# Down projections as block products in Strassen's way, with the outputs summed in SBUF

## The reference

```
def swiglu(x, w_gu, w_down):
    g, u = jnp.split(x @ w_gu, 2, axis=-1)
    return (jax.nn.silu(g) * u) @ w_down
...
    f = swiglu(rmsnorm(h, g[N_FFN1_PRE]), ffn_w_gu[layer, 0], ffn_w_down[layer, 0])
    h = h + 0.5 * rmsnorm(f, g[N_FFN1_POST])
```

## Time and profile before

| | before |
|---|---|
| median of three executions | 2197.93 us |
| span of the profiled execution | 2196.3 us (its own time is not given apart from the span) |
| TensorE busy (matmul) | 2181.2 us, 99% |
| VectorE busy | 1456.1 us, 66% |
| ScalarE busy | 1127.0 us, 51% |
| weight stream and inputs | 221.44 MB, mean 101 GB/s |

### The profile page before, as it was taken

The page is one execution under the profiler, slowest core; times in us unless marked ns, Lnnn a source line. Parts: engine busy times, 40 slices in busy tenths (PEclk is TensorE's granted clock), DMA queues, the critical chain, the costliest instruction groups (busy, mean ns, idle before and its releaser), DMA issues.

```text
span 2196.3 us, 36637 instructions
## 1 busy us (share of the span) xinstructions
PE 2181.2 (99%) x13844; PEld 1944.0 (89%) x13844; DVE 1456.1 (66%) x2185; ACT 1127.0 (51%) x1881; POOL 110.4 (5%) x104
## 2 busy tenths in 40 slices
PE   9999999999999999999999999999999999999999
PEld 8999888775888899998899998887868889999987
DVE  8888636788666598874388885345266656888732
ACT  6555524476554565563365554245345546555531
POOL 0000000675000000000000000000000000000000
PEclk9999999999999999999999999999999999999999
DMA  4332332221452233332323323322214422333322
GB/s 164 105 105 95 115 106 63 77 77 49 144 165 79 74 115 105 105 105 96 115 87 105 105 95 115 115 81 87 96 36 138 155 79 77 103 105 105 110 99 78
DMA packets 61953, 221.44 MB, mean 101 GB/s; under 512 B 7953, under 2 KB 8081, under 8 KB 61858
## 3 DMA queue, kind: packets, MB, share of 16 engines
q1 hardware_dynamic: 57456, 208.69, 28.9%
q10 hardware_dynamic: 4402, 11.46, 1.5%
HBM read 218.03 MB, written 2.10 MB: 100 GB/s over the span
## 4 chain that ended last, share of the span: by engine, by line
PE 93%; DVE 4%; ACT 1%; POOL 1%; issue 1%; DMA 0%; DVEq 0%; POOLq 0%
PE ps L2099 12%; PE ps L2100 12%; PE ps L2101 12%; PE ps L2195 11%; PE ps L2197 11%; PE ps L2196 11%; PE ps L479 6%; PE ps L480 6%; PE ps L481 6%; PE ps L2035 1%; DVE e_sc L1768 1%; DVE e_max L1767 1%; DVE e_sc L1783 1%; PE ps L2583 0%; PE ps L2560 0%
## 5 line engine op out<-in xcount | busy, mean ns | idle before, releaser
L417 DVE TENSOR_TENSOR w_lo<-w_raw,w_hi 128x1024 fp32r<-128x1024 f32 x204 | 252.5, 1241 | 358.2 <-ACT w_hi L412 357.3
L412 ACT ACTIVATE w_hi<-w_raw 128x1024 fp32r<-128x1024 f32 x210 | 221.6, 1057 | 311.4 <-PE ps L2197 225.4
L2099 PE MATMUL ps<-t_hi,w_hi 128*128 128x256 f32 x1280 | 362.3, 283 | 0.0
L2100 PE MATMUL ps<-t_lo,w_hi 128*128 128x256 f32 x1280 | 362.2, 283 | 0.0
L2101 PE MATMUL ps<-t_hi,w_lo 128*128 128x256 f32 x1280 | 362.2, 283 | 0.0
L2099 PE MATMUL ps<-x_hi,w_hi 128*128 128x256 f32 x960 | 271.7, 283 | 0.0
L2100 PE MATMUL ps<-x_lo,w_hi 128*128 128x256 f32 x960 | 271.7, 283 | 0.0
L2101 PE MATMUL ps<-x_hi,w_lo 128*128 128x256 f32 x960 | 271.7, 283 | 0.0
L1490 DVE TENSOR_TENSOR w_lo<-f,w_hi 128x1024 fp32r<-128x1024 f32 x152 | 186.2, 1225 | 124.0 <-ACT w_hi L840 124.0
L479 PE MATMUL ps<-x_hi,w_hi 128*128 128x256 f32 (+1 forms) x736 | 250.8, 341 | 1.6 <-DVE x_lo L1367 0.9
L480 PE MATMUL ps<-x_lo,w_hi 128*128 128x256 f32 (+1 forms) x736 | 246.0, 334 | 0.0
(11 more groups left out here) (352 smaller groups left out, 4317.8 us busy)
## 6 DMA issues: line engine op xcount, KB each, us to landing
w_raw<-in_wstream SPq DMA_DIRECT2D x310, 512.0 KB, 3.3
w_raw_odd<-in_wstream SPq DMA_DIRECT2D x80, 512.0 KB, 3.3
tmp<-in_post_gains ACTq DMA_DIRECT2D x8, 512.0 KB, 5.1
gain_bc<-in_gains ACTq DMA_DIRECT2D x7, 512.0 KB, 3.8
h<-in_x SPq DMA_DIRECT2D x4, 512.0 KB, 5.7
c_mem<-in_mem ACTq DMA_DIRECT2D x2, 1024.0 KB, 5.8
out_dram<-h SPq DMA_DIRECT2D x3, 512.0 KB, 2.7
c_gain<-in_mem_gains ACTq DMA_DIRECT2D x2, 512.0 KB, 7.5
```

The source lines that it names most:

```text
L412: nc.scalar.activation(weights(v)[0], raw(v), ACT.Copy).then_inc(w_hi_ready, 1)
L417: nc.vector.tensor_tensor(wl, raw(v), wh.bitcast(f32), ALU.subtract).then_inc(w_ready, 1)
L2099: nc.tensor.matmul(dst, wh[:, at], xh[:, b, :], start=first, stop=False, skip_group_check=True)
L2100: nc.tensor.matmul(dst, wh[:, at], xl[:, b, :], start=False, stop=False, skip_group_check=True)
```

## The change

The first 12 of the 22 inner blocks are treated as a two by two block matrix: tokens in two halves of 256 (tiles 0 and 1, tiles 2 and 3), inner blocks in two halves of six, output columns in two halves of 512. Seven products of sums of blocks take the place of eight products. The other ten blocks are multiplied as before. In all a down stage has 31 units (21 for the seven products, 10 for the rest) where it had 22.

(Line numbers from here on are those of the changed kernel.) VectorE forms the sums: four sums over `act_raw` of 128x1536 (L1875, L1958, L1965, L1978) and twelve weight sums of 128x1024 (L1933, L1939, L1945, L1950). Units 0 to 30 are split as before, and a block product's activations are split with its unit, as 128x512 (`down_split`, L1894 and L1899). Three of the seven products are kept once and used for two or more outputs: ScalarE copies four accumulators from PSUM to `f` (`hold`), and VectorE adds the final accumulators to them there, in five sums (`sum_c`, L1905). Afterwards `post_square` and `store_half` read `f` in place of PSUM.

SyncE makes 34 loads of 512 KB in a down stage in place of 22, into ten raw places; six of these lie in the memory of `x_hi` and `x_lo` and can be loaded only when the gate and up stage has read its inputs. Ten of the loads stand in a row with few waits between them.

The late units are gone. Tiles 0 and 1 are complete together, before the last 72 matmuls of the stage; tile 2 and tile 3 end with units 28 to 30. VectorE and ScalarE split units 29 and 30, and the first four units of the next part, between the steps of the tiles' tail.

```diff
+HALF_K = 6
+DQ = HALF_K // 2
...
-    "ffn": [("gate_up", 2 * FT), ("down", FT)],
+    "ffn": [("gate_up", 2 * FT), ("down", 7 * DQ + 2 * (FT // 2 - 2 * DQ))],
...
+            d_x = early.enter_context(nc.sbuf_tensor("d_x", [P, 8, UW], f32))
...
+            d_a = part_sb("d_a", [P, 9, 4, SEQ // 2], f32r)
+            w_raw_odd = part_sb("w_raw_odd", [P, 2, UW])
...
+        FROM_RAW = {0: (0, 1), 1: (1, 1), 2: (2, 1), 3: (3, 1), 4: (X4, 1), 5: (X5, 1), 8: (1, 2), 11: (X4, 2),
+                    14: (0, 3), 15: (1, 3), 16: (2, 3), 20: (X4, 3), 21: (2, 4), 22: (X6, 3), 23: (3, 4), 24: (1, 4),
+                    25: (X5, 4), 26: (0, 5), 27: (X4, 4), 28: (X6, 4), 29: (3, 5), 30: (2, 5)}
+        FROM_T1, FROM_T2 = {6: 0, 9: 1, 13: 2}, {7: 0, 10: 1, 12: 2}
+        FROM_T3, FROM_T4 = {17: 0, 18: 1, 19: 2}, {28: 0, 29: 1, 30: 2}
+        A_OF = {0: (0, 0), 1: (2, 0), 2: (4, 0), 3: (6, 0), 4: (8, 0), 5: (10, 0), 6: (0, 1), 7: (0, 0), 9: (2, 1),
+                10: (2, 0), 12: (4, 0), 13: (4, 1), 17: (0, 1), 18: (2, 1), 19: (4, 1), 20: (6, 0), 22: (8, 0),
+                24: (10, 0), 28: (6, 1), 29: (8, 1), 30: (10, 1)}
+        A_SLOT = {k: (0, 3, 7, 1)[n % 4] for n, k in enumerate(sorted(A_OF))}
...
+                sp.wait_ge(w_ready, u0 + 2 * FT - 3 + 1)
+                load(0, B11)
+                load(1, B11 + 1)
+                sp.wait_ge(w_ready, u0 + 2 * FT - 1 + 1)
+                load(2, B11 + 2)
+                load(3, B21)
+                sp.wait_ge(prod, 5 * (SEVENS[i] + FT))
+                load(X4, B21 + 1)
+                load(X5, B21 + 2)
+                load(KEPT, B11)
+                load(X6, B12)
+                load(KEPT + 1, B11 + 1)
+                load(KEPT + 2, B11 + 2)
+                split(0)
+                load(0, B22)
+                split(1)
+                load(1, H0)
+                split(2)
+                load(2, B12 + 1)
+                split(3)
+                load(3, B22 + 1)
...
@@ ScalarE, norm(i) behind a down stage @@
+                elif parts[i - 1][0] == "ffn":
+                    u0 = U[i, UNITS[parts[i][0]][0][0]]
+                    post(i, 0)
+                    down_split(i - 1, 29)
+                    square(0)
+                    post(i, 1)
+                    down_split(i - 1, 30)
+                    square(1)
+                    split_hi(act, u0)
+                    post_square(i - 1, 0, 2)
+                    post_square(i - 1, 0, 3)
+                    upper(0)
+                    split_hi(act, u0 + 1)
+                    post_square(i - 1, 1, 2)
...
@@ VectorE, norm(i) behind a down stage @@
+                elif parts[i - 1][0] == "ffn":
+                    u0 = U[i, UNITS[parts[i][0]][0][0]]
+                    post(i, 0)
+                    update(i, 0)
+                    down_split(i - 1, 29)
+                    scale(0)
+                    post(i, 1)
+                    update(i, 1)
+                    down_split(i - 1, 30)
+                    scale(1)
+                    sum_c22(i - 1)
+                    split_lo(dve, u0)
+                    half_sums(i - 1, 2, 4)
+                    store_half(i - 1, 0, 2)
+                    store_half(i - 1, 0, 3)
+                    lower(0)
+                    sum_c21(i - 1, 2)
+                    split_lo(dve, u0 + 1)
+                    lower(1)
+                    post(i, 2)
+                    split_lo(dve, u0 + 2)
+                    update(i, 2)
+                    sum_c21(i - 1, 3)
+                    post(i, 3)
+                    split_lo(dve, u0 + 3)
+                    update(i, 3)
+                    scale(2)
+                    scale(3)
+                    lower(2)
...
@@ VectorE @@
+            def down_split(i, k):
+
+                v = U[i, "down"] + k
+                dve.wait_ge(w_hi_ready, v + 1)
+                if k in A_OF:
+                    hi, lo = split_a(k)
+                    nc.vector.tensor_tensor(lo, act_part(*A_OF[k]), hi.bitcast(f32), ALU.subtract)
+                elif k in PLAIN_A:
+                    raw_a, hi, lo = plain_a(PLAIN_A[k])
+                    nc.vector.tensor_tensor(lo, raw_a, hi.bitcast(f32), ALU.subtract)
+                wh, wl = weights(v)
+                nc.vector.tensor_tensor(wl, down_source(k), wh.bitcast(f32), ALU.subtract).then_inc(w_ready, 1)
+
+            def sum_c(i, b, tiles, half, kept):
+
+                dve.wait_ge(d_kept, 4 * nffn[i] + kept)
+                place = f[:, tiles, half * SEQ:(half + 1) * SEQ]
+                nc.vector.tensor_tensor(place, ps[:, b, :], place, ALU.add).then_inc(d_c, 1)
...
+                dve.wait_ge(d_s, c0 + 1)
+                read(2)
+                nc.vector.tensor_tensor(a11, a21, a11, ALU.subtract).then_inc(d_s, 1)
+                down_split(i, 4)
+                first_form(0, X6, 1)
+                down_split(i, 5)
+                second_form(0, 0, 2)
+                dve.wait_ge(d_s, c0 + 2)
+                read(5)
+                nc.vector.tensor_tensor(a12, a12, a11, ALU.subtract).then_inc(d_s, 1)
+                first_form(1, 2, 2)
+                down_split(i, 6)
+                second_form(1, 3, 2)
+                down_split(i, 7)
+                down_split(i, 8)
+                read(6)
+                first_form(2, X5, 2)
+                down_split(i, 9)
+                second_form(2, X6, 2)
+                for k in range(10, 14):
...
+                for k in range(26, 29):
+                    down_split(i, k)
+                dve.wait_ge(d_full, 2 * nffn[i] + 1)
+                sum_c(i, slice(0, 2), slice(0, 2), 1, 2)
...
@@ TensorE @@
+                pe.wait_ge(g_sum, 2 * (s0 + FT - 2) + 3)
+                unit(0)
+                strassen(0, 6, start=True).then_inc(w_free, 1)
...
+                unit(6)
+                strassen(6, 0, start=True).then_inc(w_free, 1)
+                held(1)
+                unit(7)
+                strassen(7, 6).then_inc(w_free, 1)
+                unit(8)
+                plain(8, 0, (0, 1), (4, 5))
+                plain(8, 0, (2, 3), (2, 3), start=True).then_inc(w_free, 1)
...
+                unit(25)
+                plain(25, 2, (0, 1), (0, 1))
+                unit(26)
+                plain(26, 3, (0, 1), (0, 1))
+                unit(27)
+                plain(27, 4, (0, 1), (0, 1), stop=True).then_inc(d_full, 1)
+                plain(25, 2, (2, 3), (6, 7)).then_inc(w_free, 1)
+                plain(26, 3, (2, 3), (6, 7)).then_inc(w_free, 1)
+                plain(27, 4, (2, 3), (6, 7), stop=True).then_inc(w_free, 1)
+                unit(28)
+                strassen(28, 2, (0,))
+                unit(29)
+                strassen(29, 2, (0,))
+                unit(30)
+                strassen(30, 2, (0,), stop=True).then_inc(d_full, 1)
+                if i + 1 < NP:
+                    turn_x(i + 1, 0)
+                strassen(28, 2, (1,)).then_inc(w_free, 1)
+                strassen(29, 2, (1,)).then_inc(w_free, 1)
+                if i + 1 < NP:
+                    turn_x(i + 1, 1)
+                strassen(30, 2, (1,), stop=True).then_inc(w_free, 1)
 
             def output(i, seg, nu, src_hi, src_lo, halves=(0, 1), tile_ready=None):
 
```

More of the change, by code:

```diff
@@ L229, in trunk @@
         u_sum = sem("u_sum")
-        act_ready = sem("act_ready")
+        d_in = [sem(f"d_in{n}") for n in range(10)]
+        d_s = sem("d_s")
+        d_t = sem("d_t")
+        d_kept = sem("d_kept")
+        d_full = sem("d_full")
+        d_c = sem("d_c")
         o_full = sem("o_full")
@@ L477, in three, with o_half @@
+        def o_half(i, s, t):
+            return 1 - s if parts[i][0] == "ffn" and t >= 2 else s
+        NOUT = [i - nffn[i] for i in range(NP)]
+        SUMMED, n = [], 0
+        for i in range(NP):
+            first, both = (1, 2) if parts[i][0] == "ffn" else (1, 1)
+            SUMMED.append((n + first, n + both))
+            n += 0 if feeds_selection(i + 1) else both
         def three(dst, wh, wl, xh, xl, start, stop):
@@ L705, in post_mean @@
                 else:
-                    act.wait_ge(half_ssq, sum(not feeds_selection(k) for k in range(1, i + 1)))
-                    act.wait_ge(o_sq, TT * (2 * i - 1) + t + 1)
+                    act.wait_ge(half_ssq, SUMMED[i - 1][t // 2])
+                    act.wait_ge(o_sq, o_index(i - 1, 1, t) + 1)
                     bias = stat[:, i, t:t + 1]
@@ L787, in norm @@
                     whole(1)
+                    whole(2)
+                    upper(3)
+                    whole(3)
+                elif parts[i - 1][0] == "ffn":
[12 more added lines that the diff above has]
+                    post_square(i - 1, 1, 2)
+                    upper(1)
+                    post_mean(i, 2)
+                    split_hi(act, u0 + 2)
+                    post(i, 3)
+                    split_hi(act, u0 + 3)
+                    whole(0)
+                    square(2)
+                    whole(1, (0,))
```

(15 more changed lines are left out.)

423 lines of the change are left out of this document (354 added, 69 removed).

## The result

The changed kernel takes **2205.76 us** (median of 6 runs, 2203.65 to 2210.36) against 2197.94 before (6 runs, 2197.74 to 2198.49): a ratio of 1.0039, 95% interval 1.0027 to 1.0050. It is slower, by 7.8 us, and its runs spread over 6.7 us where those of before spread over 0.8. The forecast was 2193.2, the range ended at 2201. The profiled execution has a span of 2203.5 us at a mean granted clock of 0.994.

What follows compares the result with a forecast made beforehand. The prediction took TensorE, busy 99% of the span, to bound the kernel. Of 32.6 us saved, 24.3 were given back and 3.6 went to the clock, leaving 4.7: 2197.9 - 4.7 = 2193.2 us, range 2187 to 2201.

Steps and rivals of the forecast that it cites:

- What the change removes: TensorE in the four down stages: 36 of 528 matmuls fewer per stage, 8.15 us each, 32.6 us in all.
- First units: Start of each down stage: TensorE waits 0.4 us for unit 6 and 0.15 for unit 7, 0.5 per stage.
- Loads: Row of loads at a down stage's start: no cost up to 1.43 us each; ninth there at 12.5, needed at 13.7.
- Rival 3: First units' sums wait for loads: each 0.1 us per load over 1.43 costs 0.9 us per stage; chance 0.12.
- Tail behind part 0: End of the first down stage: TensorE waits 1.6, 1.6 and 5.7 us, so the stage's gain is 0.0.
- Tail behind parts 3 and 4: Ends of these down stages: TensorE's waits, first units included, come to 7.0 us, gain 1.1 us each.
- Part 7: Last down stage, with no next part: 119.3 us long against 125.3 before, gain 6.0 us.
- The clock: Behind the three third-transpose gaps: the granted clock falls, costing 1.2 us each, 3.6 us in all.
- rival 4: Low clock lasts twice as long, or also follows 1.6 us waits: 3.4 us per tail, 2199.8 us; chance 0.18.
- The sum: Whole kernel: 32.6 us saved, 24.3 given back, 3.6 for the clock, 4.7 left; span 2191.6, median 2193.2 us.

Runs made afterwards that it cites:

- last version: Changed kernel with post gains' load later, third unit's first half earlier, tail reordered, unit 29's split moved, and C12 (an output quarter) finished tile by tile: 2174.20 us.
- The fillers: Unused matmuls ahead of the third tile's transposes behind parts 0, 3 and 4, added to the changed kernel with the post gains' load late: 2194.92 us.

## Why the prediction was wrong, point by point

- **What the change removes**, 144 matmuls, 32.6 us: right. The last version keeps 23.7 us of it.
- **First units**, 0.5 us per stage: right for VectorE's own work. With the gain load late, the early waits are 0.6 and 0.8 us in two stages and 0.2 in two (tile-by-tile kernel). The 128x1536 sum took 1.67 us from start to start (243.81 to 245.48, L1958) against the 1.68 by the slope.
- **Loads: the step that failed.** "The loads cost nothing up to 1.43 us each" counted the weight loads in SP's queue and no other. The post gains' load on ScalarE's queue falls between them, and the weights that VectorE needed came 1.09 us late. The ninth load of the row, reckoned at 12.5 us into the stage, is what VectorE waits for until 15.65. With the gains late it is still 14.13, against a sum that could have begun at 13.7, just as predicted. So of the 3.1 us by which the load is late, 1.5 are the post gains', about the place of one more load, and 1.6 belong to the row of weight loads itself. Measured, TensorE waits 2.3, 1.2, 1.2 and 2.0 us for 0.5 each; the load's price is 5.6 us in the changed kernel and 6.4 in the last version. Rival 3 named the right place, the sums waiting for the row of loads. By the same reckoning (a start at -1.2, 2.0 for the first, nine loads) the weights alone came at 1.48 us each, past the border of 1.43, and with the post gains among them at 1.65. Why the weights alone took 1.48 and not the 1.3 of the opening stays open.
- **Tail behind part 0**: right. Waits of 1.5, 1.6 and 5.5 us at unit 30, first half unit and third transpose against 1.6, 1.6 and 5.7; the chain 32.9 us against 32.75. It began 3.6 us late, by the early wait (2.3 for 0.5) and the low clock behind it (1.7 us lost).
- **Tail behind parts 3 and 4**: near. Predicted 0.7 + 1.3 + 4.5; measured 0.5 + 1.8 + 2.8 and 0.5 + 1.8 + 4.3.
- **Part 7**: 121.5 us against 119.3 predicted; 1.5 of the 2.2 us is the early wait.
- **The clock: the second step that failed**, in size. I took 1.2 us for each of three gaps. The rows give 9.5 us of lost work in five stretches: 7.8 in the four at the tails, where I had 3.6, and 1.7 behind an early wait, where I had allowed for none. The fillers measured 5.2 us for the three tails with the load late. My reason for 1.2 and not 1.7, that part of the slow stretch lies in the gap, is true of part 0 (6.8 us low, 3.4 of them in the wait) and of part 4 (6.8 us low, 1.3 of them in the wait). But those stretches were twice as long as the one in the earlier trace rows, and behind part 3 a second one came, 0.7 us behind a first half unit that had waited 1.8 us. Both are what rival 4 named. The fillers' kernel kept a granted clock of 1.00, 2.4 GHz, by work that nobody uses. The rule of the Trainium skill (TensorE: Matmul & The Clock Gate, Part 1: The HAM clock gate), that the throttled state is the default and activity lifts it, agrees with that.
- **The sum.** 2203.5 against the 2191.6 of the working is 11.9 us: early waits +4.7, clock +5.9, tail waits -1.6; that leaves 2.9. The fall at 526.3 us that the kernel before has and this execution has not counts 1.7 the other way, so 4.6 us have to be placed. About 2.5 of them lie around the seven waits for a unit, which cost TensorE more than the idle time that the profile gives. One of 1.2 us, in part 3:

```profile
999.85 0.39 PE L2556 MATMUL ps<-w_hi,d_a 128*128 128x512 f32 x1
1001.49 0.47 PE L2554 MATMUL ps<-w_hi,d_a 128*128 128x512 f32 x1 [1.25 <-DVE w_lo L1899]
1001.79 0.39 PE L2555 MATMUL ps<-w_lo,d_a 128*128 128x512 f32 x1
```

From start to start that is 1.64 us, and 0.30 to the next, where two matmuls without a wait take 0.45: 1.5 us lost for an idle time of 1.25. Over this whole stage the starts lose 2.5 us, and its two waits are 1.7. The other 2 us lie between the stages, and their cause stays open. The forecast had been a balance with 4.7 us left of 32.6, so each miss was as large as the result. Rival 4 alone (2199.8) and the early waits together make 2204.5, close to 2205.8, but in part by luck: rival 4 charges the three tails 10.2 us, and the rows give 7.8.
- The run-to-run spread was not foreseen. It is 6.7 us in the changed kernel, 4.5 with the load late, 1.4 in the four runs of the last version. Falls of the clock may make it (waits of 2.3 and 2.4 us were followed by one in some stages and not in others), but that is not shown: one execution of each kernel was profiled, and the kernel with fillers and the late load, which has no low stretch in mid-kernel, still spreads over 3.2 us.

## What to carry to other kernels

When products are saved, look where the sums that replace them land: here it was where TensorE has least to do beside them. List what the other engine does between the last product and the first use; start that chain at the first finished tile, not at the last, and give TensorE independent work ahead of its wait. Before trusting a margin on a burst of loads, list every queue that issues in that stretch; a load that is not needed until later belongs behind the burst. A wait of TensorE cost more than its length here, through the clock: 5.2 us behind three gaps. And when a split or a load is moved up, look first at which slot it waits for, and at what latency it had been covering.

## What the runs showed that was not expected

- The low clock came in stretches of 3.4 and of 6.8 us, also twice with 6.8 us at full clock between (1102.2 and 1112.5 us), and once behind a wait of 2.3 us.
- Two edits of the order that each look neutral cost 5.4 and 11.8 us: VectorE's row is a chain over ScalarE's squares and TensorE's slots. In it, unit 30's split filled a wait of 1.22 us and cost nothing for that long.
- A load of 512 KB on another queue, once in each of four stages, cost 6.4 us in all, because the engine that it delayed feeds TensorE. Over its eight issues it landed after 7.6 us in the median; with the four of the down stages behind the burst, after 4.0.
